# A 31-tap depthwise convolution moved from two engines to VectorE alone

## What is computed

```python
h = rmsnorm(x, norm_mix_pre)
proj = h @ w_in
conv_in, q, k, v, g_conv, g_att = split(proj)       # 2*512, 512, 512, 512, 1024, 1024 columns
u = glu(conv_in)                                    # 512 channels
u = causal_depthwise_conv(u, conv_dw_w, conv_dw_b)  # 31 taps for each channel
u = silu(layernorm(u, conv_ln_g, conv_ln_b))
conv_out = u @ w_conv_branch + b_conv_branch
att_out = stick_breaking_attention(q, k, v) @ w_att_branch
merged = sigmoid(g_conv) * conv_out + sigmoid(g_att) * att_out
x = x + rmsnorm(merged @ w_out, norm_mix_post)
# then a feed-forward part
```

## Time and profile before

| | |
|---|---|
| median of 3 executions | 2318.79 us (2318.73 to 2321.55) |
| the profiled execution | 2317.88 us, span 2316.2 us |
| mean granted clock of TensorE | 0.969 |
| PE, DVE, ACT, POOL busy | 92%, 60%, 43%, 12% of the span |
| taps on DVE (L2029) | 90 records, 89.6 us |
| POOL's multiplies and additions (L1299, L1300) | 30 and 30 records, 65.1 and 43.5 us |

### The profile page before, as it was taken

The page is one execution under the profiler, slowest core; times in us unless marked ns, Lnnn a source line. Parts: engine busy times, 40 slices in busy tenths (PEclk is TensorE's granted clock), DMA queues, the critical chain, the costliest instruction groups (busy, mean ns, idle before and its releaser), DMA issues.

```text
span 2316.2 us, 43135 instructions
## 1 busy us (share of the span) xinstructions
PE 2125.0 (92%) x16736; PEld 1659.7 (72%) x16736; DVE 1385.9 (60%) x2170; ACT 1004.1 (43%) x1773; POOL 280.3 (12%) x242
## 2 busy tenths in 40 slices
PE   6989999978888887989999999878899988999998
PEld 4767777767777766867788877556666766787876
DVE  7667777766666644455544555599755655434345
ACT  5655555546665653232322222321677324323243
POOL 4220000012222231000000000296000000000000
PEclk8999999989999998999999999899999999999998
DMA  3345555634323212323333333122210222333322
GB/s 106 109 127 167 166 167 166 176 88 96 94 68 77 68 40 86 96 73 94 88 100 94 95 93 97 49 62 73 82 37 28 64 82 64 100 91 91 100 86 78
DMA packets 395950, 215.16 MB, mean 93 GB/s; under 512 B 85136, under 2 KB 374312, under 8 KB 395816
## 3 DMA queue, kind: packets, MB, share of 16 engines
q1 hardware_dynamic: 395608, 213.18, 31.8%
q10 hardware_dynamic: 208, 0.06, 0.0%
HBM read 181.68 MB, written 31.52 MB: 92 GB/s over the span
## 4 chain that ended last, share of the span: by engine, by line
PE 69%; DVE 17%; ACT 9%; issue 5%; SPq 1%; DMA 0%; ACTq 0%; DVEq 0%
PE bank L1584 17%; PE bank L1586 17%; PE bank L1585 17%; PE bank L540 3%; DVE dconv L2029 3%; DVE w_lo L1766 3%; ACT w_hi L1317 1%; PE bank L517 1%; PE bank L548 1%; PE bank L449 1%; PE bank L491 1%; PE bank L463 1%; PE bank L906 1%; PE bank L897 1%; ACT rstd L1326 1%
## 5 line engine op out<-in xcount | busy, mean ns | idle before, releaser
L1584 PE MATMUL bank<-xl,w_hi 128*128 128x512 f32 x1680 | 680.5, 405 | 30.7 <-DVE xl L1771 10.4
L1586 PE MATMUL bank<-xl,w_hi 128*128 128x512 f32 x1680 | 660.9, 393 | 0.0
L1585 PE MATMUL bank<-xl,w_lo 128*128 128x512 f32 x1680 | 659.4, 393 | 0.0
L1317 ACT ACTIVATE w_hi<-w_raw 128x1024 fp32r<-128x1024 f32 x280 | 293.8, 1050 | 427.4 <-PE bank L1586 427.4
L1766 DVE TENSOR_TENSOR w_lo<-w_raw,w_hi 128x1024 fp32r<-128x1024 f32 x280 | 347.1, 1240 | 125.0 <-ACT w_hi L1317 116.8
L1584 PEld LDWEIGHTS bank<-xl,w_hi 128*128 128x128 f32 x1680 | 316.8, 189 | 136.0 <-issue 42.2
L1585 PEld LDWEIGHTS bank<-xl,w_lo 128*128 128x128 f32 x1680 | 317.1, 189 | 73.2 <-issue 7.4
L1586 PEld LDWEIGHTS bank<-xl,w_hi 128*128 128x128 f32 x1680 | 316.9, 189 | 69.4
L1584 PE MATMUL bank<-xh,w_hi 128*128 128x512 f32 x480 | 200.9, 419 | 45.0 <-DVE w_lo L1766 32.9
L1586 PE MATMUL bank<-xh,w_hi 128*128 128x512 f32 x480 | 194.6, 405 | 0.0
L1585 PE MATMUL bank<-xh,w_lo 128*128 128x512 f32 x480 | 194.6, 405 | 0.0
(11 more groups left out here) (327 smaller groups left out, 3108.9 us busy)
## 6 DMA issues: line engine op xcount, KB each, us to landing
w_raw<-in_a_w_in SPq DMA_DIRECT2D x64, 512.0 KB, 4.0
w_raw<-in_b_w_in SPq DMA_DIRECT2D x64, 512.0 KB, 4.0
w_raw<-in_w_ffn_up SPq DMA_DIRECT2D x44, 512.0 KB, 3.8
w_raw<-in_w_in SPq DMA_DIRECT2D x36, 512.0 KB, 3.7
w_raw<-in_a_w_out SPq DMA_DIRECT2D x16, 512.0 KB, 4.1
w_raw<-in_b_w_out SPq DMA_DIRECT2D x16, 512.0 KB, 4.0
w_raw<-in_w_ffn_down SPq DMA_DIRECT2D x16, 512.0 KB, 4.0
d_g<-sq SPq DMA_DIRECT2D x16, 256.0 KB, 2.1
```

Source lines behind the costliest of these rows:

```text
L1317: A(w_hi[0:rows, slot, 0:nkb, 0:ncol], w_raw[0:rows, slot, 0:nkb, 0:ncol], ACT.Copy).then_inc(s_hi, 1)
L1584: mm(outp, wh, xlo, start=start, stop=False)
L1585: mm(outp, wl, xhi, start=False, stop=False)
L1586: return mm(outp, wh, xhi, start=False, stop=stop)
```

## The change

GpSimd's convolution goes, with its semaphore. All four tiles are on VectorE, 124 taps: tiles 0 and 1 alternating to their end, then tiles 2 and 3. A gated unit (j = 2, 3) and each query, key or value unit is followed by eight taps, not six. The two gate steps keep up to six. The sum of the tiles waits for all 124.

```diff
--- before.py
+++ after.py
@@ -366,7 +366,7 @@
         s_vt = sem("v_turned")
         s_vtok = sem("v_turned_copied")
         s_tap = sem("tap_added")
-        s_tap0 = sem("gpsimd_channels_convolved")
+
         s_dc = sem("depthwise_conv_summed")
         s_lnm = sem("layernorm_sum_made")
         s_cen = sem("layernorm_centered")
@@ -1292,13 +1292,6 @@
             gp.wait_ge(s_spill, SPILL_MIX + SPILL_TILE * CI)
             recurrence_gpsimd(gp, o)
 
-            gp.wait_ge(s_gluok, 1)
-            y = dconv[:, 0, :]
-            o(gt.tensor_scalar(y, glu[:, 0, 0:T], col("conv_dw_w_2", 0), col("conv_dw_b_2", 0), ALU.mult, ALU.add))
-            for tap in range(1, TAPS2):
-                o(gt.tensor_scalar(tapped[:], glu[:, 0, tap:tap + T], col("conv_dw_w_2", tap * CT), None, ALU.mult))
-                ins = gt.tensor_tensor(y, y, tapped[:], ALU.add)
-                ins.then_inc(s_tap0, 1) if tap == TAPS2 - 1 else o(ins)
 
         @block.scalar
         def _(act):
@@ -2014,11 +2007,7 @@
             norm(3, "norm_mix_pre_2", split(X_H3, xh, DK), xT2)
             def taps():
 
-                a = [(1, n) for n in range(TAPS2)] + [(3, n) for n in range(TAPS2)]
-                b = [(2, n) for n in range(TAPS2)]
-                order = a[:6]
-                for n in range(6, len(a)):
-                    order += a[n:n + 1] + b[n - 6:n - 5]
+                order = [(2 * pair + a, n) for pair in range(CT // 2) for n in range(TAPS2) for a in range(2)]
                 for n, (j, tap) in enumerate(order):
                     y, w = dconv[:, j, :], col("conv_dw_w_2", tap * CT + j)
                     if tap == 0:
@@ -2036,7 +2025,7 @@
                 dve.wait_ge(s_unit, n0 + 1)
                 V.tensor_copy(glu[:, j, PAD2:], bank[0][:]).then_inc(s_free[0], 1)
                 w_low(n0 + 2, 0)
-                for _ in range(6 if j >= 2 else 0):
+                for _ in range(8 if j >= 2 else 0):
                     next(tap)
                 dve.wait_ge(s_unit, n0 + 2)
                 V.tensor_scalar(rstd[:, j % 2, :], bank[1][:], CLAMP, None, ALU.max).then_inc(s_free[1], 1)
@@ -2056,7 +2045,7 @@
                 else:
                     ins = V.tensor_copy(v_ch[n - 2 * AT], src)
                 ins.then_inc(s_free[n % 2], 1)
-                for _ in range(6):
+                for _ in range(8):
                     next(tap, None)
             def gate2(n):
 
@@ -2075,8 +2064,7 @@
             def layer_norm(step):
 
                 if step == 0:
-                    dve.wait_ge(s_tap0, 1)
-                    dve.wait_ge(s_tap, (CT - 1) * TAPS2)
+                    dve.wait_ge(s_tap, CT * TAPS2)
                     o(V.tensor_tensor(acc[:], dconv[:, 0, :], dconv[:, 1, :], ALU.add))
                     V.tensor_tensor(acc[:], acc[:], dconv[:, 2, :], ALU.add).then_inc(s_dc, 1)
                     dve.wait_ge(s_dc, 1)
```

## The result

| | before | after |
|---|---|---|
| median | 2318.76 us (4 runs, 2317.36 to 2321.55) | 2302.89 us (4 runs, 2300.47 to 2304.60) |
| ratio | 1 | 0.9929, 95% interval 0.9912 to 0.9947 |
| the profiled execution, its span | 2317.88, 2316.2 us | 2301.74, 2300.0 us |

The change saves 15.9 us, 0.7%. The forecast of 2306.0 had the direction, the mechanism and the place, but was 3 us too high, and the measurement lies at the lower edge of the range (2302.9 by the median, 2302.3 by the ratio, against 2302.5).

The account below looks back on a forecast made before the run. VectorE was taken to bound the query, key and value units; POOL's removal and 0.665 us taps start the mean matmul 12.2 us earlier, 2317.88 - 12.2 = 2305.7, stated as 2306.0 us, range 2302.5 to 2311.5.

Parts of the forecast that it names:

- VectorE is the bound from 1498 to 1617: In the query, key and value units VectorE sets the pace: 8.21 us a turn against 5.49 for a PE unit.
- Taps at 0.665: All 124 VectorE taps take 0.665 us each after the change, with 0.78 as the upper bound.
- GpSimd as the cause: Taps took 1.08 us because GpSimd's SBUF reads and VectorE's two-input instructions exclude each other.
- Rival 3: Slow taps come from the stretch itself, not GpSimd: turns of 10.4 us, total 2354 us; chance 0.03.
- Third gated unit: clamp at 1508.4: In the j = 2 unit, eight taps (5.3 us) bring the next step, L2042, to 1508.4; old 1510.70.
- First turn at 1524.0, end of the turns at 1608.7: Query, key and value units: start 1524.0 (old 1528.53), twelve turns of 7.06 us, end 1608.7 (old 1621.91).
- Additions done at 1623.5, PE late by 1.7 us: After the gate steps additions end at 1623.5 (old 1635.5); PE, through at 1621.8, stands 1.7 us before the mean matmul.
- Rival 1: PE's low clock in the query, key and value turns costs 0.4 us per slow unit, 5.3 for twelve: 2311; chance 0.08.
- Sum: Whole kernel: 2317.88 - 12.2 = 2305.7, or 2306.6 by the median of three runs; stated as 2306.0 us.
- the gain up to the mean matmul: The layer norm's mean matmul starts at about 1623.6 instead of 1635.9: gain 12.3, say 12.2 us.
- everything outside of that stretch: After the layer norm waits are on engines, not clock times, so the rest should move up as it is.
- The range: Whole kernel: 2302.5 to 2311.5 us, up for the clock rival, 3.5 down for a clock stretch less and cheaper tap zeros.

Follow-up runs that it names:

- fill7: Changed kernel with twelve taps moved into VectorE's idle time in the gated units, seven instead of eight behind each query, key or value unit: 2297.51 us.
- fill_act: Changed kernel with twelve taps moved into VectorE's idle time in the gated units, and the twelve PSUM copies made by ScalarE: 2296.43 us.
- fill7_act: fill7 with the twelve query, key and value PSUM copies made by ScalarE instead of VectorE: 2290.15 us, 0.9886 of the kernel before.
- the three kernels above: Changed kernel plus GpSimd's 61 old instructions: 2338.56 us; changed kernel plus 180 GpSimd fills: 2303.80; kernel before, GpSimd's tile 0 cut to one tap: 2285.84.

## Why the prediction was right or wrong, point by point

- *VectorE is the bound from 1498 to 1617, though PE is busy for 92% of the span.* Right. fill7, fill_act and fill7_act took their share out of each turn in full (6.37, 6.44 and 5.78 us).
- *Taps at 0.665.* Right: 0.66. Three quiet alternating taps in the earlier trace rows were a thin base for 124; they turned out to be typical.
- *GpSimd as the cause.* Right, by the three kernels above. Rival 3 is out.
- *Third gated unit: clamp at 1508.4.* 1507.41. Of the 1.0 us, 0.5 are ahead of the stretch (1476.65 against 1477.16), 0.4 are two first taps at 0.46 (0.91 us for both in the chain) that I had priced at 0.665.
- *First turn at 1524.0, end of the turns at 1608.7.* 1523.04 and 1607.06. 84.0 us for twelve turns against 84.7: two more cheap first taps, and 7.04 for 7.06.
- *Additions done at 1623.5, PE late by 1.7 us.* 1621.75, and PE stood for 1.45. The mean matmul started 1.8 us earlier than worked out, 0.5 of it from ahead.
- *Rival 1, the low clock in the turns.* It didn't come, in 24 turns of two traces; the gaps are 1.2 to 1.35 us, shorter still than the 1.6 expected. Its price is also added up loosely: twelve times 0.4 is 4.8 us, not 5.3. What I had missed is that the old kernel had something to lose there: 1.5 us in one of its two traces.
- *Sum, the step that failed.* The mechanism was right; two terms of the sum had the wrong size. The first is the gain up to the mean matmul, priced at 12.2 us: from the same starting point it measured 13.4 in the first pair of traces and 14.0 in the means of two pairs. Of the 1.2 us in the first pair, 0.8 are the four first taps at 0.46 us, priced like all others at 0.665, and the rest are hundredths in the turns and gate steps. The second is everything outside of that stretch, put at nothing ("the rest should move up as it is"): 0.5 us ahead and 2.2 behind in the first pair. 13.4 + 0.5 + 2.2 = 16.1, which is 2317.88 - 2301.74. The 2.7 us outside are not the change's, as far as the traces show: the changed kernel's second trace had the tail 0.8 us longer than the old kernel's first. Why both comparisons of medians still give 16 us, 2 more than the traces have in the stretch, stays open.
- *The range.* It gave 3.5 us downwards for cheap first taps and for clock stretches. The untouched head alone varies by 8 us over twelve traces, and the old kernel's stretch by 1.6 between two. Below the forecast it should have had at least the cheap first taps (0.8) and a low stretch of each kernel (1.5 to 2 each), some 5 us.

## What to carry to other kernels

Work on an idle GpSimd is not free when it reads SBUF beside a VectorE that is the bound: here 61 of its instructions cost the stretch twice as much (28 us) as the same taps on VectorE in the better order (14 us). Two independent chains, alternating, were worth 0.13 us on each in-place 128 x 512 instruction, and without that the move would have brought nothing. Before filling an engine's idle time, look at where the work was taken from: only out of a stretch in which that engine is the bound does it count.

## What the runs showed that I had not expected

- The panel's low half (128 x 1024, two SBUF inputs) doubled from 1.14 to 2.2 us beside GpSimd's reads when the turns fell in step with them: five turns of 11.03 us to a hundredth alike.
- GpSimd's fills, which read nothing, left 120 two-input taps alone and lengthened one-input ones by 44% (536 to 772 ns, median of four).
- The first 1477 us, identical in all kernels of this study, took 1472.7 to 1480.9 us.
